# The products of the one-hot rows in the expert selection go from the Vector engine to GpSimd, between the gathers of rounds 11 to 15

## What is computed

```python
def block(xb):                                   # 128 tokens
    q = (xb @ w_q).reshape(BLK, PEER_HEADS, PEER_QDIM)      # 8 heads
    s1 = einsum('thd,hkd->thk', q[..., :64], sub_keys[:, 0])
    s2 = einsum('thd,hkd->thk', q[..., 64:], sub_keys[:, 1])
    v1, i1 = lax.top_k(s1, 16); v2, i2 = lax.top_k(s2, 16)
    cand = (v1[..., :, None] + v2[..., None, :]).reshape(BLK, PEER_HEADS, 256)
    sc, ci = lax.top_k(cand, 16)
    e = take_along_axis(i1, ci // 16) * 128 + take_along_axis(i2, ci % 16)
    g = softmax(sc)
    a = gelu(einsum('thkd,td->thk', u[e], xb)) * g
    return einsum('thk,thkd->td', a, v[e])
```

## Time and profile before

| | |
|---|---|
| median of 3 runs | 3063.28 us (3061.88 to 3075.15) |
| the profiled execution | 3063.9 us, its span 3062.2 us |
| TensorE busy | 2385.2 us, 78% |
| DVE busy | 2157.2 us, 70% |
| ScalarE busy | 1212.5 us, 40% |
| GpSimd busy | 1300.3 us, 42% |
| moved by DMA | 1176.87 MB, mean 384 GB/s |

### The profile page before, as it was taken

One profiled execution on the slowest core, in us unless ns is written; L12 is line 12 of the kernel. 1 busy time (PEld: TensorE's weight loads), 2 busy tenths in 40 slices (PEclk: granted clock), 3 DMA queues, 4 the chain that ended last, 5 costly groups with the idle time before them and its releaser, 6 DMA issues.

```text
span 3062.2 us, 31998 instructions
## 1 busy us (share of the span) xinstructions
PE 2385.2 (78%) x7648; PEld 1272.7 (42%) x7648; DVE 2157.2 (70%) x4995; ACT 1212.5 (40%) x3525; POOL 1300.3 (42%) x1186
## 2 busy tenths in 40 slices
PE   7548887788877888776986779777887869875677
PEld 6425453354434545242552435333453425422222
DVE  2486578665886658858688775977669686886644
ACT  2123434443433344434444453434534344432333
POOL 0123424444344443434443554344434444345574
PEclk9768999889998999988998989899899989988899
DMA  5469999999999999999999999999999999999998
GB/s 202 154 245 396 405 387 400 412 393 418 384 405 411 396 411 377 403 422 415 408 396 376 411 421 400 359 383 417 413 406 367 370 421 395 396 371 423 422 422 361
DMA packets 164354, 1176.87 MB, mean 384 GB/s; under 512 B 18944, under 2 KB 19200, under 8 KB 22352
## 3 DMA queue, kind: packets, MB, share of 16 engines
q0 software_dynamic: 147456, 1073.81, 85.8%
q1 hardware_dynamic: 16720, 101.03, 8.2%
HBM read 1170.57 MB, written 4.19 MB: 384 GB/s over the span
## 4 chain that ended last, share of the span: by engine, by line
DMA 19%; PE 18%; DVE 12%; issue 8%; POOL 4%; ACT 3%; POOLq 0%; DVEq 0%; ACTq 0%; SPq 0%
DMA ring<-in_uv,pick_now 18%; PE acc L1407 11%; POOL ring L540 4%; DVE ring L901 4%; PE ps L1214 3%; PE ps L1203 1%; DMA xc<-h 1%; PE ps L1342 1%; DVE arena L852 1%; DVE arena L856 1%; DVE arena L844 1%; ACT diag L1136 0%; DVE arena L792 0%; DVE arena L804 0%; PE ps L1212 0%
## 5 line engine op out<-in xcount | busy, mean ns | idle before, releaser
L1407 PE MATMUL acc<-ring,diag 128*128 128x512 f32 x3328 | 1680.1, 653 | 560.9 <-ACT diag L1136 554.5
L540 POOL DMA_INDIRECT ring<-in_uv,pick_now x1024 | 1243.6, 1214 | 1604.7 <-PE acc L1407 1266.7
L901 DVE CUSTOM_DVE_ANT_0 ring<-ring,h_now 128x1024 f32<-128x1024 f32 x1024 | 1232.0, 1222 | 567.0 <-DMA ring<-in_uv,pick_now 555.2
L1407 PEld LDWEIGHTS acc<-ring,diag 128*128 128x128 f32 x3328 | 660.5, 207 | 1483.1 <-ACT diag L1136 790.5
L1123 ACT ACTIVATE gelu<-dots 128x1 f32<-128x1 f32 x1024 | 205.5, 201 | 1243.1 <-DVE dots L901 1193.6
L1136 ACT ACTIVATE diag<-ident,coef 128x128 f32<-128x128 f32 x832 | 334.1, 402 | 87.9 <-PE acc L1407 50.4
L1126 ACT ACTIVATE coef<-gate,gelu 128x1 f32 (+1 forms) x1024 | 301.5, 294 | 110.2
L895 DVE SCALAR_TENSOR_TENSOR side<-ring,coef,side 128x1024 f32<-128x1024 f32 x192 | 246.2, 1283 | 115.5 <-ACT coef L1126 113.5
L1214 PE MATMUL ps<-resident,actT 128*128 128x256 f32 x768 | 179.8, 389 | 0.0
L1214 PEld LDWEIGHTS ps<-resident,actT 128*128 128x128 f32 x768 | 145.8, 193 | 36.0 <-issue 17.5
L1214 PE MATMUL ps<-stream,actT 128*128 128x256 f32 x576 | 136.0, 392 | 16.8 <-ACT actT L976 9.3
(11 more groups left out here) (182 smaller groups left out, 1414.5 us busy)
## 6 DMA issues: line engine op xcount, KB each, us to landing
stream<-in_strips SPq DMA_DIRECT2D x68, 1024.0 KB
resident<-in_strips SPq DMA_DIRECT2D x16, 1024.0 KB, 17.4
ring<-in_uv,pick_now POOLq DMA_INDIRECT x1024
arena<-in_keys SPq DMA_DIRECT2D x8, 512.0 KB
xc<-in_x SPq DMA_DIRECT2D x4, 512.0 KB, 6.4
h<-arena SPq DMA_DIRECT2D x4, 512.0 KB, 10.6
xc<-h SPq DMA_DIRECT2D x4, 512.0 KB, 9.2
out<-arena SPq DMA_DIRECT2D x4, 512.0 KB, 9.8
```

Source lines behind the costliest of these rows:

```text
L540: pool.indirect_dma_start(ring[:, i, :], None, tables[layer], bass.IndirectOffsetOnAxis(ap=pick_now[:, half, i:i + 1], axis=0),).then_inc( ...
L901: dve.tensor_tensor_reduce(ring[:, i, 0:D], ring[:, i, 0:D], h_now[:], 1.0, 0.0, ALU.mult, ALU.add, dots[:, i:i + 1]).then_inc(dotted, 1)
L1407: m = pe.matmul(acc[:, b * 512:(b + 1) * 512], diag[:, i % 4, :], ring[:, i, D + b * 512:D + (b + 1) * 512], start=(r0 == 0 and i == TENSO ...
```

## The change

The `is_equal` of both halves of a part moves ahead to the end of `pick{j}5`, the tile `onehot` is doubled to hold both, and the new event `pair{j}` says that they are there. GpSimd does the four products of the part (`hot`), after it has issued the gathers of a round named in `HOT_AT`: part 0 after round 11, part 1 after round 12, part 2 after round 14, part 3 after round 15. It says `hot{j}`, for which DVE waits at `pick{j}7` before it makes the two sums. For the first block GpSimd does all four parts before its first gather. The table `AT` stays as it is.

```diff
+HOT_AT = {"gla": (11, 12, 14, 15), "swa": (11, 12, 14, 15)}
...
-        onehot = area(2560, PART * TOPK, TOPK)
+        onehot = area(2560, 2, PART * TOPK, TOPK)
...
+            def hot(prep, part):
+
+                said_by(pool, "dve", prep, f"pair{part}")
+                alone(pool, passed["pool"])
+                step.restart()
+                for half in range(2):
+                    for i in range(PART):
+                        o = onehot[:, half, i * TOPK:(i + 1) * TOPK, :]
+                        ins = pool.tensor_tensor(
+                            o, o, topf[:, half * HEADS_P + part * PART + i, :].rearrange(
+                                "p (o j) -> p o j", o=1).to_broadcast([P, TOPK, TOPK]), ALU.mult)
+                        if (half, i) != (1, PART - 1):
+                            step.mark(ins)
+                step.settle()
+                ins.then_inc(said["pool"], 1)
...
+                    if after and any(2 * pair + half in HOT_AT[after.kind] for pair in pairs for half in range(2)):
+                        for pair in pairs:
+                            for half in range(2):
+                                fetch(pair, half)
+                                if after and 2 * pair + half in HOT_AT[after.kind]:
+                                    hot(after, HOT_AT[after.kind].index(2 * pair + half))
+                    else:
+                        with pool.Fori(pairs[0], pairs[-1] + 1) as pair:
+                            for half in range(2):
+                                fetch(pair, half)
 
             pool.wait_ge(started, 1)
-            with pool.Fori(0, BLOCKS) as s:
-                stage(s, Prep("gla", s), 0)
-            with pool.Fori(BLOCKS, STAGES) as s:
-                stage(s, Prep("swa", s - BLOCKS), 1)
+            for part in range(PARTS):
+                hot(Prep("gla", 0), part)
+            with pool.Fori(0, BLOCKS - 1) as s:
+                stage(s, Prep("gla", s), 0, Prep("gla", s + 1))
+            stage(BLOCKS - 1, Prep("gla", BLOCKS - 1), 0, Prep("swa", 0))
+            with pool.Fori(BLOCKS, STAGES - 1) as s:
+                stage(s, Prep("swa", s - BLOCKS), 1, Prep("swa", s - (BLOCKS - 1)))
+            stage(STAGES - 1, Prep("swa", BLOCKS - 1), 1, None)
...
+                for half in range(2):
+                    ins = dve.tensor_tensor(
+                        onehot[:, half],
                         abf[:, half, hs, :].rearrange("p h (k o) -> p (h k) o", o=1).to_broadcast(
                             [P, PART * TOPK, TOPK]),
                         iota16[:].rearrange("p (o j) -> p o j", o=1).to_broadcast([P, PART * TOPK, TOPK]),
+                        ALU.is_equal)
+                    if half == 0:
+                        step.mark(ins)
+                say(prep, f"pair{part}", ins)
...
-                expert(0)
                 yield at[f"pick{part}7"]
-                expert(1)
+                said_by(dve, "pool", prep, f"hot{part}")
+                alone(dve, passed["dve"])
+                for half in range(2):
+                    step.mark(dve.tensor_reduce(ef[:, half, hs].rearrange("p h k -> p (h k)"), onehot[:, half], AX,
+                                                ALU.add))
+                step.settle()
```

More of the change, by code:

```diff
@@ L101 @@
     "act": ["sq2", "sqrt2", "h2T", "pq0", "pq1", "gexp0", "pq2", "gexp1", "pq3", "gexp2", "gexp3"],
-    "dve": ["x2", "var2", "h2"] + [f"{w}{j}" for j in range(PARTS) for w in ("seen", "gshift", "experts")],
+    "dve": ["x2", "var2", "h2"] + [f"{w}{j}" for j in range(PARTS) for w in ("seen", "gshift", "pair", "experts")],
+    "pool": [f"hot{j}" for j in range(PARTS)],
 }
@@ L113 @@
         "dve": ["var", "h", "absx", "bdiff", "qd", "kf", "attn", "state0", "state1", "ovar", "o"] + SELECT["dve"],
+        "pool": SELECT["pool"],
     },
@@ L244, in build @@
         h_taken = sem("h_taken")
-        said = {"pe": sem("pe_said"), "act": sem("act_said"), "dve": sem("dve_said")}
+        said = {"pe": sem("pe_said"), "act": sem("act_said"), "dve": sem("dve_said"),
+                "pool": sem("pool_said")}
         own = {"pe": sem("pe_step"), "act": sem("act_step"), "dve": sem("dve_step"), "pool": sem("pool_step")}
@@ L520, in _, with stage, fetch @@
             pool.memset(pick_now[:, 1, :], 0).then_inc(started, 1)
-            def stage(s, prep, layer):
+            def hot(prep, part):
[12 more added lines that the diff above has]
+                ins.then_inc(said["pool"], 1)
+            def stage(s, prep, layer, after):
+                def fetch(pair, half):
+                    n = (s * (ROUNDS // 2) + pair) * 2 + half
+                    step.restart()
+                    step(pool.tensor_copy(
+                        pick_now[:, half, :],
+                        pick[:, bass.ds((s * (ROUNDS // 2) + pair) * (2 * SLOTS)
+                                        + (half * SLOTS - layer * BLOCKS * PICKS), SLOTS)]))
+                    for i in range(SLOTS):
+                        pool.wait_ge(used[i], n + 1)
+                        alone(pool, passed["pool"])
+                        pool.indirect_dma_start(
+                            ring[:, i, :], None, tables[layer],
+                            bass.IndirectOffsetOnAxis(ap=pick_now[:, half, i:i + 1], axis=0),
+                        ).then_inc(got[i], 16)
                 for part in range(PARTS):
@@ L526, in stage @@
                     alone(pool, passed["pool"])
[L527 to L543, removed]
@@ L545, in _ @@
-            pool.wait_ge(started, 1)
-            with pool.Fori(0, BLOCKS) as s:
-                stage(s, Prep("gla", s), 0)
-            with pool.Fori(BLOCKS, STAGES) as s:
-                stage(s, Prep("swa", s - BLOCKS), 1)
+                    pairs = range(part * ROUNDS // (2 * PARTS), (part + 1) * ROUNDS // (2 * PARTS))
+                    if after and any(2 * pair + half in HOT_AT[after.kind] for pair in pairs for half in range(2)):
[8 more added lines that the diff above has]
+                                fetch(pair, half)
@@ L848, in expert @@
                         iota16[:].rearrange("p (o j) -> p o j", o=1).to_broadcast([P, PART * TOPK, TOPK]),
[L849 to L856, removed]
+                        ALU.is_equal)
+                    if half == 0:
+                        step.mark(ins)
+                say(prep, f"pair{part}", ins)
+                cols = bass.ds(prep.p * PICKS + part * (PICKS // PARTS), PICKS // PARTS)
                 yield at[f"pick{part}6"]
```

## The result

The changed kernel takes 3231.79 us (median of 4 runs, 3230.11 to 3234.42) against 3062.65 of the kernel before (4 runs, 3061.88 to 3075.15): ratio 1.0543, 95% interval 1.0515 to 1.0571. It is slower by 169 us. The forecast was slower, 3155, and its range ended at 3200.

The account below looks back on a forecast made before the run. It took DMA time for the gathers plus holes to bound the kernel. Prologue 18, swa stages 44 and gla stages 30 made +92 on the profiled 3063.9 us, 3156, or 3155 against the median; range 3105 to 3200.

Parts of the forecast that it names:

- Prologue, +18: Before the first gather: GpSimd does all four `hot` first, first gather issued at about 189; +18 us, ends 12 and 23.
- Nothing later should absorb it: Prologue: its loss stays to the end, as DMA is the pace, but for some of the holes.
- GpSimd's product: Products on GpSimd: 0.62 us each, a `hot` of four 2.8 us, ends 1.5 and 3.8.
- slowed by DVE: Rival: each GpSimd product waits out one dot, a `hot` beside dots 5 us longer; +35, 3190 us; chance 0.10.
- A swa stage, +11: Stages 3 to 6: GpSimd waits for `pair0` and `pair1`, DMA idles; +11 us each, ends 7 and 16, four stages +44.
- Given back: the 12 products of parts 1 to 3, 5 us on a DVE that is full in this stretch, so DVE ends 9 late: Swa stage: credit of 5 us for products taken from DVE, against round 13 landing 14 us late.
- that close later: Swa stage: credit for some holes closing later; 20.3 us new, less 4.1 already there, less these, gives 12.
- the ring covers most: Swa stage, parts 2 and 3, behind rounds 14 and 15: they cost GpSimd a `hot` and a short wait, mostly covered.
- unchanged: Stage 7, which prepares nothing: the profile after should show it still at 315 us.
- A gla stage, +10: Stages 0 to 2: DVE waits for `hot0` and `hot2`, delayed 10 and 7 us; +10 each, ends 5 and 17, three stages +30.
- the ring of 8 ... covers a part, and some of the hole of 4.8 us ... was there already: Gla stage: credit against the 17 us of delays, from up to 19.9 us of queued work and a hole in 440 to 460.
- the stalls add with no cover: Rival: 17 per gla stage, 20 per swa stage, 20 in the prologue, together 151; 3215 us; chance 0.08.

Follow-up runs that it names:

- e1: Changed kernel, but the first block's products stay on DVE as in the kernel before: 3223.96 us, ratio 1.0517 to the kernel before.
- e5: Changed kernel with its order and waits, but DVE makes the products ahead of `pair` and GpSimd only passes the word on: 3210.49 us, ratio 1.0482.
- e4: Changed kernel, but parts 0 and 2 of all gla preparations, the first block's too, are done on DVE: 3195.15 us, ratio 1.0418.
- e2: Changed kernel, but parts 0 and 1 of the swa preparations are done on DVE, 2 and 3 on GpSimd: 3151.9 us, ratio 1.0284.
- e6: Changed kernel, but swa `hot0`, `hot1` a round later, sums and index in the next part's piece 4, part 3 and first block on DVE: 3092.36 us.
- e10: e6 with every product on GpSimd made twice, the second time into a spare place: 3128.14 us, ratio 1.0201 to the kernel before.

## Why the prediction was wrong

Direction, places and chains were right, the size was not: the terms of the stages were credited with relief that did not come. The steps that failed are these two credits, from 20.3 to 11 us in a swa stage and from 17 to 10 in a gla stage; the changed kernel lost 21 to 28 and 17 to 20.

**Prologue, +18.** The size was right where it arises: 17 to 19 us at rounds 1 and 2, first gather at 188.9. "Nothing later should absorb it" is not borne out: with the prologue as before (e1) only 8 us come back at the end by the medians, 9 by the traces, not 17 or 18.

**GpSimd's product.** Right where DVE stands (2.76 us for four, forecast 2.8). Next to dots it is 4.4 to 5.4, the rival "slowed by DVE" at a third to a half of the 5 us that it had for a `hot`; all 128 average 0.92 us by the profile's group. It is an addition, not the cause: some 22 of the 169 us (e5).

**A swa stage, +11.** The chain came as worked out: the first dot of round 12 5.7 us later than that of round 11 was (forecast 4.7), DMA idle for 10.0 and 10.9 us (10.6 and 9.7). The first dot of round 13 is 2064.9 - 1949.4 = 115.5 us behind, that of round 11 was 97: 18.5 us more, where 14 was forecast. Of the 4.5 between them 1.0 stood there at round 12, 1.6 is the slower `hot1`, and 0.9 the second dot of the refill, which came 3.4 us behind the first and not 2.5; 1.0 is open. Then the step that failed: "Given back: the 12 products of parts 1 to 3, 5 us on a DVE that is full in this stretch, so DVE ends 9 late". The 5 us did not come back: from round 13 to the end of the stage the dots fell another 3 behind. DVE was no longer full. Its waits for gathers in the stretch from round 13 to the end of stage 4, first before, then after:

```profile
DVE ring L901 <- DMA ring<-in_uv,pick_now: 1.7, 1, 1.7
```

```profile
DVE ring L935 <- DMA ring<-in_uv,pick_now: 17.5, 6, 8.4
```

Behind the 8.4 us of the drained ring there are 9 us of further waits: in a ring that is refilled from empty a dot waits for its gather, and the time that DVE saves goes into those waits. The other credit of that step, holes "that close later", failed as well. The windows up to the first dot of round 13 and from there to the end of the stage, first before, then after:

```profile
1904.00:1949.40 45.40, 38.16 (x167) 22.75 (x167) 40.62 (x143) 17.49 (x47) 15.79 (x16) 0.92 0.93 379
1949.40:2022.00 72.60, 54.93 (x121) 22.83 (x120) 65.95 (x203) 27.91 (x82) 30.94 (x29) 0.91 0.93 361
```

```profile
2001.00:2064.90 63.90, 48.23 (x183) 26.35 (x181) 42.52 (x149) 18.89 (x52) 22.59 (x25) 0.89 0.63 253
2064.90:2140.40 75.50, 53.09 (x108) 21.35 (x108) 61.02 (x188) 27.07 (x80) 37.74 (x37) 0.84 0.86 341
```

DMA's idle time grows by 20 us in the first stretch (3 to 24), where the prediction counted 20.3 less the 4.1 that were there, and behind it from 5 to 11: later holes opened by 5 or 6 us instead of closing by 4. DVE is busy for 81% of the second stretch instead of 91%. My own uncredited count of new holes, 20.3 us, is what parts 0 and 1 cost alone (20 to 23 a stage when they alone are on GpSimd, 20 by what goes when they alone are not). Parts 2 and 3, for which "the ring covers most", are 15 us in the four stages together, with waits of 6 to 8 us for `pair3`; the last of them makes stage 7 the 7 us longer that "unchanged" did not have.

**A gla stage, +10.** The two waits of DVE were forecast at 13 and 10 us and delays of 10 and 7; measured are 13.2 and 9.3, and the dots fall back by 10 and 7 at rounds 12 and 14. The step that failed is again the credit: "the ring of 8 ... covers a part, and some of the hole of 4.8 us ... was there already". It covered nearly nothing: 17 to 20 us a stage, against 17 without credit, and some 15 of them go when parts 0 and 2 are on DVE (e4). Nor did parts 1 and 3 give back 3: alone they cost 2 to 5. A slot is free only behind its dot, so a DVE that stands for 10 us frees none. In stage 1 DMA's idle time grows from 7 to 19 us (370.3 us at share 0.98 from round 1 to round 1', 388.5 at 0.95 after), 12 of the 18 us that are lost there; the rest is open.

**The sum.** Without credits the terms were 18 + 4 x 20.3 + 3 x 17 = 150, near the rival "the stalls add with no cover" (3215), which had 0.08 and is the one that came nearest. The rest to 169 is about what parts 2 and 3 of the swa preparations cost. That the sum fits so well is in part luck. Taken out one at a time, the swa term returns 80 us of its 81 (e2), the gla term 37 of 51 (e4) and the prologue 8 of 18 (e1), so the delays do not simply add. One edit I had at nothing, the earlier place of the comparisons; with the products beside them, all on DVE, such an order costs 19 us by itself. How much of it the comparisons alone would cost was not run.

## What to carry to other kernels

If the queue that feeds a ring also holds a wait for something else, look at what the ring still has in flight when the wait begins, and count each idle microsecond of DMA in full: time that a compute engine saves behind an emptied ring is spent waiting for the refill. When a piece of a hand-made order goes to another engine, place both sides anew, and price the new order by a run in which the work has not moved: here that order alone cost 19 to 37 us, more than the work was worth. An idle engine that issues all the gathers is no free capacity: 3.1 us more of work between its issues cost 1.6, the waits of DVE for it counted in.

## What the runs showed of the hardware

DVE and GpSimd slow each other down, both ways. From e6, four products on GpSimd and the dots beside them:

```profile
2315.38 6.77 POOL L537 TENSOR_TENSOR arena<-arena 128x256 f32<-128x256 f32 x4
```

```profile
2315.05 1.53 DVE L982 CUSTOM_DVE_ANT_0 ring<-ring,h_now 128x1024 f32<-128x1024 f32 x1
...
2316.51 1.73 DVE L982 CUSTOM_DVE_ANT_0 ring<-ring,h_now 128x1024 f32<-128x1024 f32 x1
...
2318.18 1.73 DVE L982 CUSTOM_DVE_ANT_0 ring<-ring,h_now 128x1024 f32<-128x1024 f32 x1
...
2319.84 1.73 DVE L982 CUSTOM_DVE_ANT_0 ring<-ring,h_now 128x1024 f32<-128x1024 f32 x1
```

Four products take 6.77 us instead of 2.76, and a dot 1.73 instead of 1.22: 0.3 to 0.5 us of DVE for each dot that runs beside them, so four products moved away from DVE (1.7 us there) cost it 1.8 us again when dots run.

Not every instruction of DVE is slowed. From e10, products on GpSimd, and beside them the sums of candidates (two inputs) and the searches (one input) of DVE:

```profile
2346.76 2.86 POOL L547 TENSOR_TENSOR arena<-arena 128x256 f32<-128x256 f32 x4
```

```profile
2346.72 1.16 DVE L858 TENSOR_TENSOR arena<-arena 128x256 f32<-128x256 f32 x2
2347.92 0.75 DVE L865 MAX8 arena<-arena 128x8 f32<-128x256 f32 x2
```

With GpSimd idle the two additions take 0.75 us and the two searches 0.75 as well (0.42 each by their groups in the kernel before): the former are slowed, the latter not. The GPSIMD Engine Reference of the Trainium skill (Specifications) says that GpSimd shares its access to the on-chip memory with DVE instructions that have two inputs there. The rows agree and give the price; a cast with one input grows too, from 0.26 us for two to 0.77 beside products (L846 in e6). In the kernel before, where GpSimd only issues gathers, the mean dot takes 1222 ns; over all 1024 dots of the changed kernel it is 1234.
